# Hybrid decoder layer on one Trainium2 core: ScalarE's queue sends every second tile of the second expert table

## The reference

```python
eidx = jnp.take_along_axis(cidx, sel, axis=-1)        # 8 heads x 16 experts per token
g = jax.nn.softmax(top, axis=-1)
a = jax.nn.gelu(jnp.einsum('nd,nhkd->nhk', hx, u_tab[eidx]).astype(jnp.float32), approximate=False)
w = (g * a).astype(hx.dtype)
return jnp.einsum('nhk,nhkd->nd', w, v_tab[eidx])
```

## Time and profile before

| | |
|---|---|
| median of three runs | 1189.4 us (1187.7 to 1193.85) |
| the profiled execution, its own time | 1190.0 us |
| its span, first to last instruction | 1188.3 us |
| mean granted TensorE clock | 0.99 of full speed |
| DMA traffic | 268.42 MB, mean 226 GB/s |

### The profile page before, as it was taken

One profiled execution on the slowest core, in us unless ns is written; L12 is line 12 of the kernel. 1 busy time (PEld: TensorE's weight loads), 2 busy tenths in 40 slices (PEclk: granted clock), 3 DMA queues, 4 the chain that ended last, 5 costly groups with the idle time before them and its releaser, 6 DMA issues.

```text
span 1188.3 us, 23705 instructions
## 1 busy us (share of the span) xinstructions
PE 1158.0 (97%) x8356; PEld 1083.0 (91%) x8356; DVE 852.3 (72%) x1594; ACT 629.2 (53%) x1207; POOL 622.2 (52%) x549
## 2 busy tenths in 40 slices
PE   6999999997999999999999999999999999999998
PEld 5689989985799999999999999999898988988988
DVE  5577556654587599999967887886876666766666
ACT  5445454442254454555556777755555555555554
POOL 4402134443000088777778786330377777777760
PEclk9999999898999999999999999999999999999999
DMA  8663448867575357677776666789899999988994
GB/s 306 212 215 104 126 120 241 289 216 236 167 277 178 107 170 187 159 172 186 177 186 170 162 162 163 210 257 325 301 334 319 308 305 309 302 296 308 311 312 151
DMA packets 141735, 268.42 MB, mean 226 GB/s; under 512 B 51504, under 2 KB 80240, under 8 KB 140912
## 3 DMA queue, kind: packets, MB, share of 16 engines
q1 hardware_dynamic: 100176, 207.82, 53.6%
q0 software_dynamic: 38720, 55.68, 18.5%
q10 hardware_dynamic: 2720, 3.40, 0.8%
HBM read 250.37 MB, written 20.62 MB: 228 GB/s over the span
## 4 chain that ended last, share of the span: by engine, by line
PE 83%; issue 6%; POOLq 3%; DVE 3%; DMA 2%; POOL 2%; ACT 1%; SPq 0%; DVEq 0%; ACTq 0%
PE ps L2271 27%; PE ps L2351 16%; PE ps L2276 14%; PE ps L2358 9%; PE ps L2395 3%; PE ps L1821 2%; PE ps L1985 2%; PE ps L1841 2%; POOLq L584 2%; PE ps L1907 1%; PE ps L2325 1%; POOL arena L585 1%; POOLq L450 1%; PE ps L1848 1%; PE ps L2301 1%
## 5 line engine op out<-in xcount | busy, mean ns | idle before, releaser
L1036 ACT ACTIVATE w_hi<-ring 128x1024 fp32r<-128x1024 f32 x280 | 296.8, 1060 | 332.6 <-issue 248.6
L1531 DVE TENSOR_TENSOR w_lo<-ring,w_hi 128x1024 fp32r<-128x1024 f32 x271 | 331.1, 1222 | 165.3 <-ACT w_hi L1036 164.0
L2271 PE MATMUL ps<-h_hi,w_hi 128*128 128x288 f32 x1088 | 294.5, 299 | 0.5 <-ACT w_hi L1036 0.5
L621 POOL DMA_INDIRECT gates<-arena x128 | 243.7, 1904 | 68.2 <-issue 45.9
L2271 PE MATMUL ps<-h_lo,w_hi 128*128 128x288 f32 x1024 | 277.0, 295 | 0.0
L2271 PEld LDWEIGHTS ps<-h_hi,w_hi 128*128 128x128 f32 x1088 | 205.0, 188 | 1.2 <-ACT w_hi L1036 1.0
L2271 PEld LDWEIGHTS ps<-h_lo,w_hi 128*128 128x128 f32 x1024 | 192.4, 188 | 0.0
L631 POOL DMA_INDIRECT arena<-in_v,aux x122 | 142.5, 1168 | 83.0 <-DVE aux L1705 35.6
L2276 PE MATMUL ps<-h_hi,w_lo 128*128 128x288 f32 x1088 | 167.3, 296 | 0.2 <-DVE w_lo L1531 0.2
L2276 PEld LDWEIGHTS ps<-h_hi,w_lo 128*128 128x128 f32 x1088 | 151.7, 188 | 0.5 <-DVE w_lo L1531 0.5
L2351 PE MATMUL ps<-h_hi,w_hi 128*128 128x432 f32 x680 | 149.2, 360 | 1.0 <-DVE h_hi L1752 0.5
(11 more groups left out here) (375 smaller groups left out, 2027.8 us busy)
## 6 DMA issues: line engine op xcount, KB each, us to landing
ring<-in_uT SPq DMA_DIRECT2D x128, 512.0 KB, 3.6
ring<-in_v SPq DMA_DIRECT2D x128, 512.0 KB, 4.9
ring<-in_wout SPq DMA_DIRECT2D x32, 512.0 KB, 3.9
ring<-in_wT SPq DMA_DIRECT2D x28, 512.0 KB, 5.6
gates<-aux SPq DMA_DIRECT2D x32, 256.0 KB, 5.8
act_kept<-arena SPq DMA_DIRECT2D x32, 144.0 KB, 4.0
ring<-in_wtok SPq DMA_DIRECT2D x8, 512.0 KB, 5.5
arena<-in_cache_slc_v POOLq DMA_DIRECT2D x64, 64.0 KB, 3.8
```

The costliest lines, as they stand in the source:

```text
L621: pool.indirect_dma_start(gates, bass.IndirectOffsetOnAxis(rt("gi")[:, P + s:P + s + 1].bitcast(U32), 0), rt("gi")[:, s:s + 1], None, comp ...
L1036: act.activation(w_hi[e % 2][:, :], ring[:, (W_O + e) % RING, :], ACT.Copy).then_inc(S["w_high"], 1)
L1531: dve.tensor_tensor(w_lo[e % 2][:, :], ring[:, (W_O + e) % RING, :], w_hi[e % 2][:, :].bitcast(F32), ALU.subtract)\
L2271: last = pe.matmul(ps[:, bank, 0:NT], w_hi[e % 2][:, k * P:(k + 1) * P], mov[:, k, :], start=(k == 0 and mov is mov_hi), stop=False, skip_ ...
```

## The change

SyncE sends the tiles 0 to 3 and the even ones. The odd tiles from 5 to 127 (62 of them) are sent by ScalarE: right after the rounding of tile t (t odd, from 3 on) its queue holds a wait for the low part of tile t - 2 and the issue of the load of tile t + 2. Slots, semaphores and the other work are as before.

```diff
             for t in range(PK):
-                low_done(sp, W_V + t - RING - W_O)
-                sp.dma_start(ring[:, t % RING, :], A["v"][v_tile(t)]).then_inc(ring_in[t % RING], 16)
+                if t < RING or t % 2 == 0:
+                    low_done(sp, W_V + t - RING - W_O)
+                    sp.dma_start(ring[:, t % RING, :], A["v"][v_tile(t)]).then_inc(ring_in[t % RING], 16)
                 if t in (0, 4):
                     keep_activations(30 + t // 4)
...
             for t in range(2, PK):
                 w_high(E_V + t)
+                if t % 2 and RING <= t + 2 < PK:
+                    low_done(act, E_V + t - 2)
+                    act.dma_start(ring[:, (t + 2) % RING, :], A["v"][v_tile(t + 2)]).then_inc(ring_in[(t + 2) % RING], 16)
                 if t + 1 < PK:
                     mov_high(t + 1)
```

## The result

The changed kernel takes 1206.03 us in the median of three runs (1202.01 to 1208.43), against 1189.4. The ratio is 1.0136, interval 1.0109 to 1.0164. Its profiled execution took 1208.43 us, with a span of 1206.8 (before: 1190.0 and 1188.3). TensorE's clock is the same (0.989). The kernels were run side by side again in two later groups, each group on one chip; there the kernel before took 1199.9 and 1206.1 us, and the changed one 1.0011 and 1.0032 of it. The changed kernel stays near the same time (1206.0, 1201.9 and 1209.6 us in its three medians); it is the kernel before that took 1189.4 us once and 1199.9 to 1206.1 us in the three later groups. On which chip or chips the first pair ran is not on record, so the 1.4% was measured once and did not come back. The third group of experiments looks into this.

What follows compares the result with a forecast made beforehand. TensorE was taken to bound the kernel, busy 1158.0 of 1188.3 us. Loop 10.3 + start 3.5 - slack 2.0 = 11.8 us on 1190.0 gave 1201.8, or 1201 us against the median; range 1188 to 1219.

Steps and rivals of the forecast that it cites:

- The sum and the sign: Whole kernel: slower, 11.8 us on the profiled 1190.0, 1201 us against the median; chance of slower 0.61.
- One turn takes 0.97 + landing + 0.02.: Odd tiles' loop of rounding, send and landing: bounds the kernel from a landing of 4.54 us, TensorE needing 5.53.
- The window: Time from an odd tile's send to its earliest rounding: 4.91 - 0.97 = 3.9 us, down from 7.5 us.
- The landing of an odd tile: Second table's odd loads: from the 4.9 us median, less 0.18 for thinner traffic, 4.72 us.
- The price: Loop over the second table: a turn of 5.71 us, 0.18 us per pair, 10.3 us over 57 pairs.
- The start: First odd tiles, loaded behind the burst of SP's queue: 3.5 us lost, against 2.0 us of slack spent once.
- ScalarE's issues at nothing: ScalarE's 62 added issues, 21.8 us in all, were taken to cost nothing, as they fit its idle time.
- Where the time would show: Signs in the second table: over 50 us of ScalarE landing waits, odd tiles alone; tiles 13 to 127 in 323 to 330 us.
- The odd tile overtakes: Rival: ScalarE's queue brings odd landings to 4.5 us or less, so no change, 1190 to 1193 us; chance 0.33.
- Contention in full: Rival: paired sends make odd landings 5.2 us, a turn of 6.19, 38 us more, 1226 with the start; chance 0.10.

Runs made afterwards that it cites:

- The third group of experiments: Runs against the kernel before (1206.1 us): itself again 1.0008, changed kernel 1.0032, odd tiles sent by SyncE at the changed kernel's moments 1.0105, ScalarE sending before its rounding 1.0001.

## Why the prediction was right, step by step

*The sum and the sign.* 1201 was forecast, 1206.0 measured, inside the range. The mechanism is the one argued: a closed loop of landing, rounding and send that takes longer than TensorE needs for two tiles. The median that is compared, 1189.4 us, did not come back later, so it is this one pair that the forecast met.

*"One turn takes 0.97 + landing + 0.02."* This step was wrong. I read the send's place off ScalarE's next instruction; but the queue issues a load while the engine rounds, 0.01 us after the rounding's start. The turn is landing + 0.02, and the loop becomes the bound from a landing of 5.51 us on, not from 4.54. The window was 4.9 us, not 3.9.

*"The landing of an odd tile": 4.72 us taken, 5.75 measured* on average where a rounding waited for it (5.77 from send to rounding; the median of the 29 landings in the trace is 5.4). I started from the median of all loads and took some off for thinner traffic. It rose instead, while the even tiles' median fell to 4.7. The recorded median of 5.4 is a poor measure here: with it a turn would be 5.42 us, under TensorE's 5.53, and cost nothing. The mean from send to rounding is the one that adds up to the stage. The even tile in front is sent 1.6 us before (1.1 was my estimate).

*The price.* The two errors cancel: 0.97 too much in the fixed part, about as much too little in the landing. The turn was forecast at 5.71 us and measured at 329.0 / 57 = 5.77. Over 57 turns the loop costs 13.9 us (329.0 - 315.1), not 10.3. The turn as a whole came out well by luck: both of its parts were wrong by about 1 us.

*The start.* 3.5 - 2.0 = 1.5 us were forecast. Tile 13 is rounded at 867.9 in place of 863.4, 4.5 us later. Of this 1.8 us lie ahead of all that was changed: tile 0 is rounded at 829.0 in place of 827.2 (the first numbers of these rows, changed and before).

```profile
L1037 ACT ACTIVATE w_hi<-ring x13: 1042/1062/1063, 829.0 to 863.8; 128x1024 fp32r<-128x1024 f32 x13
```

```profile
L1036 ACT ACTIVATE w_hi<-ring x13: 1042/1061/1063, 827.2 to 860.9; 128x1024 fp32r<-128x1024 f32 x13
```

So the start cost 2.7 us. 13.9 + 2.7 + 1.8 = 18.4 us, which is the difference of the two profiled executions (1208.43 - 1190.0).

*ScalarE's issues at nothing.* Right: they take 0.33 us each, and with them moved one tile forward the ratio is 1.000 (0.9974 to 1.0026).

*Where the time would show.* Idle time before L1036 by landings over 50 us: 138.1. Landings in the chain over 5%: 94.6%. Tiles 13 to 127 in 323 to 330 us: 329.0. The waits are on odd tiles alone. All that is as forecast. Even tiles keep their slack: they are sent 9.0 us before their rounding. Two signs were missed: the odd roundings were to start 0.97 us + landing + 0.02 after one another with a landing of 4.6 to 4.9, and landings of 5.2 and more were named as a sign that the prediction is wrong. By that sign it failed; the time was met all the same, because the 0.97 was not there.

*The rivals.* "The odd tile overtakes" is out: its landing got longer. "Contention in full" asked for 5.2 us of landing, and that came, with 5.4; its 38 us did not, because its turn carried the 0.97 as well. (Its total was also added up wrongly: 1189.4 + 38 + 3.5 - 2.0 is 1229, not 1226.) What I did not consider at all is that the kernel before may have idle time of its own in another measurement, which takes the loss in: there the change costs 0.1 to 0.3%, and the 0.1% is not clear of none.

## What to carry to other kernels

A load that is sent behind the wait for an earlier load's landing ties the landings into a chain; compare one landing with what the bound engine needs for the tiles between, on average, and put the send ahead of that wait if it is too long. Here a send written behind an instruction of ScalarE left as that instruction began; look at the issue row before pricing the window. A cost that only eats slack showed in full where the bound engine was full and hardly at all where it had gaps, so compare the waits as well as the times, and measure the pair again.

## What the runs showed of the hardware that I had not expected

- ScalarE's queue issued its loads 0.01 us after the start of the rounding that stands in front of them in the program, and 1.09 us after it only when made to wait for its end.
- From sending a 512 KB load to its use, where a rounding waited for it: 6.2 us with the send in front less than 1 us away, 5.0 at 2.2 to 3 us, in one profile of the changed kernel. No run varied the distance alone.
- The same kernel, at the same granted clock, ran the table's tiles 13 to 127 in 315.1 us in its first profile and in 329.1 us in a later one. In the later one 33 of VectorE's low parts started 0.25 to 3.3 us after their rounding with VectorE free, in the first none. The cause stays open.
- After a gap of 6.9 us TensorE's granted clock was 0.70 in the mean of the next 7 us, and a high part took 3.25 us in place of 1.75.
